# Split-product projections that compute two output tiles at a time, their products alternating between two PSUM banks

## The reference

```
proj = hn @ w_in;  z, xbc, dt, u5, gate_a, gate_b = split(proj)
xbc  = silu(causal_conv(xbc));  y_ssd = chunked_scan(xbc, dt) ...
y_ssd = rms_norm(y_ssd * silu(z));  branch_a = y_ssd @ w_ssd_branch
glu  = s5_scan(u5) @ w_glu + b_glu
branch_b = glu[:, :D] * sigmoid(glu[:, D:])
h = x + (sigmoid(gate_a) * branch_a + sigmoid(gate_b) * branch_b) @ w_mix_out
h = h + memory_attention(rms_norm(h), K, V, w_mem_q, w_mem_o)
h = h + hier_moe(rms_norm(h))        # 4 groups x 8 experts, one group, two experts per token
```

## Time and profile before

| | |
|---|---|
| time, median of 3 runs | 1074.19 us (1073.09 to 1075.43) |
| profiled execution, span from first to last instruction | 1070.9 us |
| what lies around the span (median less span) | 3.3 us |
| PE busy | 933.7 us (87%), 6660 instructions |
| PEld busy | 627.2 us (59%) |
| DVE busy, ACT busy | 476.9 us (45%), 327.0 us (31%) |
| DMA | 297.69 MB, mean 278 GB/s |
| float32r products of 320 columns, lines 1856 to 1858 | 3 x 368, 311, 310 and 310 ns each |
| float32r products of 256 columns, lines 1867 to 1869 | 3 x 128, 291, 283 and 283 ns each |

### The profile page before, as it was taken

How to read it: one execution, slowest core, us unless ns; L and a number is a source line. 1 busy time by engine, 2 the same in 40 slices (tenths; PEclk the granted TensorE clock), 3 DMA queues, 4 the chain that set the end, 5 groups by cost and what they waited for, 6 DMA issues and landing times.

```text
span 1070.9 us, 15963 instructions
## 1 busy us (share of the span) xinstructions
PE 933.7 (87%) x6660; PEld 627.2 (59%) x6660; DVE 476.9 (45%) x801; ACT 327.0 (31%) x650; POOL 53.9 (5%) x82
## 2 busy tenths in 40 slices
PE   6999999999999999999999999767678587677484
PEld 4788478995579999988878754223223223232121
DVE  5999965667677445656565411201102020202023
ACT  4143155566476245554444431000000000000003
POOL 2601400010100000000000000000000000000000
PEclk9999999999999999999999999978878788888688
DMA  9672450345462744524699789999999999999994
GB/s 271 140 187 76 153 196 2 120 142 170 136 210 99 303 161 155 206 80 158 245 368 355 297 354 407 429 430 427 428 427 426 427 430 426 425 429 428 428 419 152
DMA packets 82051, 297.69 MB, mean 278 GB/s; under 512 B 20013, under 2 KB 29961, under 8 KB 67516
## 3 DMA queue, kind: packets, MB, share of 16 engines
q1 hardware_dynamic: 79652, 289.33, 70.0%
q0 software_dynamic: 2112, 7.28, 2.0%
q10 hardware_dynamic: 216, 0.06, 0.0%
HBM read 286.76 MB, written 9.90 MB: 277 GB/s over the span
## 4 chain that ended last, share of the span: by engine, by line
PE 68%; DMA 24%; SPq 2%; ACT 2%; DVE 2%; issue 1%; POOL 1%; DVEq 0%; ACTq 0%; POOLq 0%
DMA ring<-in_w_exp_down_dram 12%; PE bank L1474 7%; PE bank L2204 7%; DMA ring<-in_w_exp_gate_dram 7%; PE bank L1459 6%; DMA ring<-in_w_exp_up_dram 5%; PE bank L1856 5%; PE bank L1857 5%; PE bank L1858 5%; PE bank L2222 4%; PE bank L2250 3%; PE bank L1483 3%; PE bank L1747 2%; PE bank L1646 2%; PE bank L1867 2%; PE bank L1868 1%
## 5 line engine op out<-in xcount | busy, mean ns | idle before, releaser
L2204 PE MATMUL bank<-ring,work 128*32 128x512 f32 x704 | 138.5, 700 | 67.8 <-DMA work<-in_w_exp_up_dram 23.2
L2204 PEld LDWEIGHTS bank<-ring,work 128*32 128x32 f32 x704 | 34.6, 127 | 153.3 <-issue 120.4
L1856 PE MATMUL bank<-ops,usplit 128*128 128x320 f32 x368 | 114.6, 311 | 1.1 <-DVE usplit L2722 1.1
L1857 PE MATMUL bank<-ops,usplit 128*128 128x320 f32 x368 | 114.0, 310 | 0.0
L1858 PE MATMUL bank<-ops,usplit 128*128 128x320 f32 x368 | 113.9, 310 | 0.0
L2222 PE MATMUL bank<-ring,work 128*32 128x512 f32 x416 | 68.0, 721 | 40.6 <-DMA ring<-in_w_exp_down_dram 28.3
L2722 DVE TENSOR_TENSOR usplit<-ring,usplit 128x2048 fp32r<-128x2048 f32 x31 | 71.0, 2290 | 52.9 <-ACT usplit L1145 52.9
L3049 DVE TENSOR_TENSOR work<-bank,g 128x512 f32<-128x512 f32 x7 | 4.8, 692 | 200.6 <-PE bank L2250 200.6
L2204 PE MATMUL bank<-work 128*32 128x512 f32 x304 | 85.4, 694 | 0.0
L1474 PE MATMUL bank<-work,ring 128*128 128x320 f32 (+1 forms) x304 | 77.4, 412 | 0.0
L1145 ACT ACTIVATE usplit<-ring 128x2048 fp32r<-128x2048 f32 x32 | 61.5, 1921 | 40.5 <-PE bank L1858 31.6
(11 more groups left out here) (504 smaller groups left out, 1600.8 us busy)
## 6 DMA issues: line engine op xcount, KB each, us to landing
ring<-in_w_exp_down_dram SPq DMA_DIRECT2D x20, 2048.0 KB, 20.0
ring<-in_w_exp_gate_dram SPq DMA_DIRECT2D x18, 2048.0 KB, 16.0
ring<-in_w_exp_up_dram SPq DMA_DIRECT2D x16, 2048.0 KB, 19.7
ring<-in_w_in_dram SPq DMA_DIRECT2D x11, 2048.0 KB, 9.7
work<-in_w_exp_up_dram SPq DMA_DIRECT2D x8, 2048.0 KB, 28.6
work<-in_w_exp_gate_dram SPq DMA_DIRECT2D x6, 2048.0 KB, 22.1
ring<-in_w_exp_gate_dram SPq DMA_DIRECT2D x11, 1024.0 KB, 7.4
ring<-in_w_glu_dram SPq DMA_DIRECT2D x4, 2048.0 KB, 8.7
```

What stands on the lines that cost most here:

```text
L1856: nc.tensor.matmul(b[:, 0:T], wh, hi_[:, k], start=(k == 0), stop=False)
L1857: nc.tensor.matmul(b[:, 0:T], wh, lo_[:, k], start=False, stop=False)
L2204: ins = nc.tensor.matmul(psum[part][ES * x:ES * (x + 1), :], xs[i % 2][:, kk, x], wt[x][:, k], start=(kk == 0), stop=(kk == KT - 1))
```

## The change

Wherever a unit's two tiles follow each other, they are now computed together: both banks are taken at the start, and for each of the 8 input blocks the six products alternate between the two banks. The sum of each tile and the order within it stay the same. Both tiles are complete at the end of the pair, one product apart; `full` is signalled for each as its own last product ends. Paired are xbc4 to xbc11, z0 with z1, all of gb, sb, gv, gg, q2 to q7, ga but for ga4 and ga5 (between which another job stands), the first two chunks of mx, and of o in the last two units. Alone stay z2, ga4, ga5 and the chunks of o in the first two units; q0 and q1 (`queries`) are not touched. For the pair z0, z1 the job z1 moves ahead of s5o0 and s5o1 in the plan, on TensorE and on ACT.

```
-    j += ["z0", "s5o0", "s5o1", "z1"] + [f"nc{q}" for q in range(3)]
+    j += ["z0", "z1", "s5o0", "s5o1"] + [f"nc{q}" for q in range(3)]
...
             keep_z(0)
+            keep_z(1)
             got(act, "s5o0")
...
-            keep_z(1)
...
-            def proj_split(kind, m, hi_, lo_, ready=None):
+            def proj_split(kind, ms, hi_, lo_, ready=None):
-                job, u = f"{kind}{m}", unit_of(f"{kind}{m // 4}", m % 4 // 2)
-                b = take(job)
+                u = unit_of(f"{kind}{ms[0] // 4}", ms[0] % 4 // 2)
+                bs = [take(f"{kind}{m}") for m in ms]
                 pe.wait_ge(s["wlo"], u + 1)
                 for k in range(KT):
                     if ready:
                         pe.wait_ge(s[ready], k + 1)
-                    wh, wl = (v[u % 2][:, k, P * (m % 2):P * (m % 2 + 1)] for v in (uhi, ulo))
-                    nc.tensor.matmul(b[:, 0:T], wh, hi_[:, k], start=(k == 0), stop=False)
-                    nc.tensor.matmul(b[:, 0:T], wh, lo_[:, k], start=False, stop=False)
-                    ins = nc.tensor.matmul(b[:, 0:T], wl, hi_[:, k], start=False, stop=(k == KT - 1))
-                end(ins, job)
+                    wh, wl = ([v[u % 2][:, k, P * (m % 2):P * (m % 2 + 1)] for m in ms] for v in (uhi, ulo))
+                    for b, wv in zip(bs, wh):
+                        nc.tensor.matmul(b[:, 0:T], wv, hi_[:, k], start=(k == 0), stop=False)
+                    for b, wv in zip(bs, wh):
+                        nc.tensor.matmul(b[:, 0:T], wv, lo_[:, k], start=False, stop=False)
+                    for b, wv, m in zip(bs, wl, ms):
+                        ins = nc.tensor.matmul(b[:, 0:T], wv, hi_[:, k], start=False, stop=(k == KT - 1))
+                        if k == KT - 1:
+                            end(ins, f"{kind}{m}")
...
-            for m in range(KT):
+            for ms in ((0, 1), (2, 3), (4,), (5,), (6, 7)):
+                m = ms[0]
...
-            for c in range(2):
-                tok_part("mx", 0, c, mrg_hi, mrg_lo, bs[c], 0, KT - 1)
+            tok_part("mx", 0, (0, 1), mrg_hi, mrg_lo, bs, 0, KT - 1)
             pe.wait_ge(s["mrg_lo"], KT)
```

More of the change, by code:

```diff
@@ L1673, in _, with proj_halved @@
                     end(ins, f"ko{m}{hf}")
-            def proj_halved(job):
-                u, m = HALVED.index(job) // 2, HALVED.index(job) % 2
-                b = take(job)
+            def proj_halved(*jobs):
+                u = HALVED.index(jobs[0]) // 2
+                bs = [take(job) for job in jobs]
                 pe.wait_ge(s["xlo"], 1)
@@ L1694, in _ @@
             end(ins, "cs")
-            for m in range(4, CT):
-                proj_halved(f"xbc{m}")
-            proj_halved("z0")
+            for m in range(4, CT, 2):
+                proj_halved(f"xbc{m}", f"xbc{m + 1}")
+            proj_halved("z0", "z1")
             b = take("s5o0")
@@ L1709, in _ @@
             end(ins, "s5o1")
-            proj_halved("z1")
             pe.wait_ge(s["convout"], CT)
@@ L1864, in tok_part, with pairs @@
+            def pairs(m0, m1):
+                return [(m, m + 1) for m in range(m0, m1, 2)]
+            def tok_part(kind, i, cs, hi_, lo_, bs, k0, k1):
+                u = unit_of(f"{kind}0") + i
                 pe.wait_ge(s["wlo"], u + 1)
                 for k in range(k0, k1):
-                    th_, tl_ = (v[:, k, P * c:P * c + R] for v in (hi_, lo_))
-                    nc.tensor.matmul(b[0:R, 0:256], th_, uhi[u % 2][:, k], start=(k == 0), stop=False)
-                    nc.tensor.matmul(b[0:R, 0:256], th_, ulo[u % 2][:, k], start=False, stop=False)
@@ L1872, in tok_samples @@
+                    for b, tv, c in zip(bs, tl_, cs):
+                        ins = nc.tensor.matmul(b[:, 0:256], tv, uhi[u % 2][:, k], start=False, stop=(k == KT - 1))
+                        if k == KT - 1:
+                            end(ins, f"{kind}{i}{c}")
             def tok_samples(kind, i, whole):
@@ L1880, in tok_samples, with tok_split @@
                 end(ins, job)
[L1882 to L1887 removed]
+            def tok_split(kind, i, cs, hi_, lo_):
+                tok_part(kind, i, cs, hi_, lo_, [take(f"{kind}{i}{c}") for c in cs], 0, KT)
+            for ms in ((0, 1), (2, 3), (4,), (5,), (6, 7)):
+                m = ms[0]
                 if m == 4:
@@ L1898, in _ @@
                     end(nc.tensor.matmul(b[:, 0:T], ones[:, :], yr1, start=True, stop=True), "ssy")
-                proj_split("ga", m, hn_hi, hn_lo, "hn_lo" if m == 0 else None)
-            for m in range(4):
-                proj_split("gb", m, hn_hi, hn_lo)
+                proj_split("ga", ms, hn_hi, hn_lo, "hn_lo" if m == 0 else None)
+            for ms in pairs(0, 4):
+                proj_split("gb", ms, hn_hi, hn_lo)
             pe.wait_ge(s["yb_lo"], KT)
[L1903 to L1906, removed]
+            for ms in pairs(0, KT):
+                proj_split("sb", ms, yb_hi, yb_lo)
+            for ms in pairs(4, KT):
+                proj_split("gb", ms, hn_hi, hn_lo)
             pe.wait_ge(s["u5_lo"], 1)
@@ L1909, in _ @@
                 for kind in ("gv", "gg"):
-                    for m in range(4 * i, 4 * i + 4):
-                        proj_split(kind, m, *(v.rearrange("p j t c -> p t j c") for v in (u5_hi, u5_lo)))
+                    for ms in pairs(4 * i, 4 * i + 4):
+                        proj_split(kind, ms, *(v.rearrange("p j t c -> p t j c") for v in (u5_hi, u5_lo)))
             def rows_in(k):
@@ L1977, in keys @@
                     end(ins, f"kt{bb}{i}")
-            for m in range(2, 6):
-                proj_split("q", m, q_hi, q_lo)
+            for ms in pairs(2, 6):
+                proj_split("q", ms, q_hi, q_lo)
             def scores(k):
@@ L2018, in _ @@
             scores(0)
-            for m in (6, 7):
-                proj_split("q", m, q_hi, q_lo)
+            proj_split("q", (6, 7), q_hi, q_lo)
             done(pe, "q3")
```

43 lines of the change are left out of this document (24 added, 19 removed).

## The result

The changed kernel takes 1088.8 us (median, 1087.3 to 1089.9), the kernel before beside it 1074.6 us: the ratio is 1.0130 (95% interval 1.0117 to 1.0143), 14.2 us slower. I had forecast 8.4 us, 1082.6 us, and the time lies above my range, which ended at 1086. The same kernel measured again, later and beside other runs of before (e1_again), took 1085.3 us against 1074.6: 1.0116 (1.0087 to 1.0144), 10.7 us slower, which is inside the range. Both have to be explained.

The account below looks back on a forecast made before the run. TensorE bounds the first 640 us, expert weights the rest, and delays reach the end. Six waits, 1.1 + 1.0 + 0.9 + 0.9 + 1.8 + 2.7 = 8.4 us, and 0 from the banks give 1082.6 us; range 1077 to 1086.

Parts of the forecast that it names:

- rival 3: Expert weight loads run on during the pauses, so half of the 8.4 us arrives: 1078.4 us; 8%.
- Rival 1: The bank holds products up, so alternating frees up to 13.3 ns each, 21.1 us; 1069.3 us after added waits; 12%.
- xbc10: TensorE waits at this convolution-input tile for the unit split behind the preceding pair: 1.1 us.
- nc0: TensorE, after z0, z1 and the S5 transposes, waits here for all convolutions: 1.0 us.
- gv0: Wait behind the pair gb4, gb5, for emptying, S5 output rounding and DVE's rest: 0.9 us.
- gv4: Wait behind the pair gg0, gg1, for tanh, merge steps, rounding and the split: 0.9 us.
- gv6: Wait behind the pair gg2, gg3, whose steps stand ahead of the needed split: 1.8 us.
- mx00: First w_mix_out product waits for merged tile 6, now as late as its neighbour: 2.7 us.
- 0 at q2 to q7: Nothing lost at the second tile of the query pairs q2 to q7: 0 us.
- rival 4: More waits than six, at q, mx and o: 2 to 4 us more, 1085 to 1087 us; 5%.
- 3.3 us around the span: Time outside the profiled span, added to the predicted span of 1079.3 us to reach 1082.6 us.
- rival 2: Nothing waits, as the order on ACT and DVE leaves more room than counted: 1074.2 us; 5%.

Follow-up runs that it names:

- e8: The kernel before with 62 additional unused products ahead of the wait for mrg_lo, to delay everything from w_mix_out on by busy work; 1085.7 us, ratio 1.0100.
- e9: The changed kernel with only ga, gb0 to gb3, sb, q2 to q7, mx and o still in alternating pairs; 1075.1 us, ratio 1.0009.
- e2: The changed kernel with tile after tile instead of alternation, the first tile of a pair still signalled late; 1085.6 us, ratio 1.0107.
- e11: The changed kernel with only xbc4 to xbc11 and z0, z1 in pairs, z1 moved ahead of s5o0; 1078.6 us, ratio 1.0045.
- e12: The delayed kernel of e8 with two more unused products in the router, so that TensorE hardly pauses there; 1083.1 us, ratio 1.0077.
- e4: The changed kernel with 20 additional unused products in TensorE's pause ahead of w_mix_out; 1083.2 us, ratio 1.0086.
- e13: The changed kernel with the 20 additional products of e4 and the two router products of e12; 1084.0 us, ratio 1.0086.
- e7: The changed kernel with only gb4 to gb7, gv and gg paired, odd xbc and z tiles using their even neighbours' weights; 1572 us, a total that says nothing.
- e15: The kernel before with the two additional router products of e12; 1075.2 us, ratio 1.0002.
- e5_before: The kernel before, unchanged, measured once more with a profile; 1074.1 us, ratio 0.999.

## Why the prediction was right or wrong

- *What bounds the kernel, and that delays pass 1:1.* Right. Stretch V is within 0.6 us of before wherever no fall reaches into it from the router or lies longer in it; e8 refutes rival 3.
- *0 from the banks.* Right. 864 alternating products change nothing (e9), and the whole loss is there without alternation (e2). Rival 1 is refuted. The trace after has 147 ns again, now across banks at every product, so the 13.3 ns over the 133.3 of 320 columns at 2.4 GHz are not the bank's. The Trainium skill, page "TensorE: Matmul & The Clock Gate", section "Wait — 56ns, not 53.3ns?", gives N / 2.4 + 2.5 ns, which is 135.8 ns for 320 columns; the trace does not agree, before or after.
- *xbc10 1.1, nc0 1.0.* Right: 1.1 and 0.9; alone 2.04 (e11).
- *gv0 0.9, gv4 0.9, gv6 1.8.* Right: 1.0, 1.0, 1.7.
- *mx00 2.7.* Right as a wait (3.36 instead of 0.69 us), and it belongs to these pairs: with gg4 to gg7 alone it is 1.13.
- *0 at q2 to q7.* Off by 0.6 us (III); it is rival 4, smaller than I had made it.
- *Sum 8.4 us, forecast 1082.6.* **Here it failed.** The sum has no term for the granted clock. I had priced every product at 146.7 or 120 ns, as at 1.00, and never asked whether it stays there once TensorE pauses for 3.4 us. It doesn't: 1.3 to 1.5 us go where the fall lasts 3.4 us, 2.6 where it lasts 6.8 (II). The second missing term is the router, later than before and at times at half clock: 3.1 us in the profile of after, 2.0 in that of e8, 2.6 by the medians of e8 and e12. Together with the 0.6 at q they bring TensorE to the experts 13.1 us later, the start of the execution apart, where I had written 8. With the waits, the 0.6 and no fall the kernel takes 1083.2 to 1084.0 us (e4, e13), where the waits alone put it. That e1_again's 1085.3 us lies inside the range is luck: the range reached there for more waits, and 1.5 us of what it has above 1082.6 are the clock's.
- *3.3 us around the span.* The sum does not need it, but it is not what its name says: where an execution has both numbers, the time is 1.7 to 2.9 us more than the span. The profiled execution of before was an early one (xbc4 at 193.73).
- *Nothing waits* (rival 2): refuted.

The first of these terms was open to me: the row of the pause was in my own working. The page "TensorE: Matmul & The Clock Gate" of the Trainium skill, section "Why this matters for your kernels", asks to leave no long idle gaps of TensorE between bursts of products, because the clock is taken back behind them. The trace agrees at w_mix_out, where five pauses of 3.34 to 3.36 us had a fall each. By the same advice the router, whose longest pause is 0.79 us, would be safe; after, e7 and e8 show falls there, so the measurement goes beyond this advice.

## What to carry to other kernels

Where TensorE's products already follow each other without a gap, as here, alternating banks gained nothing, and completing two tiles together moves all the emptying behind the pair: count the chain of ACT and DVE from there. Price a new pause of TensorE twice, once for its length (here 2.7 us) and once for the products behind it at half the clock (here 1.3 to 2.6 us). Look also at light stretches further on, like the router here: behind a delay the clock fell there in some executions. Useless products into a free bank, in a wait that can't be avoided, can save more than they cost; here they saved 1.5 to 2 us.

## What the hardware showed beyond that

- The falls were 3.4 to 13.7 us long (the longest among the experts), and for the same pause (3.34 to 3.36 us) once 6.8 and in four profiles 3.4. How often each comes over many executions is not known from one profile per kernel.
- The router's fall came with a longest pause of 0.79 us, in a stretch of short products: behind the pause come products of 96, 64, 32, 64 and 32 columns, two of 256 and twelve of 128. It stands in 3 of 13 profiles. With two more products in the stretch there was none in four (e12 to e15), which so few profiles do not prove.
- The time to xbc4, in code that is the same everywhere, was 193.5 to 196.9 us. In before and e5_before, both without a fall there, it differs by 2.0 us: 1.2 us have arisen by 28 us, the rest between 76 and 82 us, where TensorE pauses for 2.53 instead of 1.75 us. Why is open.
